# Norms of the differential heads and of the latents: sums in 128x4 columns, rows spread by PE at places of their own in the order of products

## What is computed

```
oa = diff_attention(a_q, a_k, a_v, lam, rel_bias)          # 4 heads of 128 values
oa = rms_norm(oa, da_subln[l]) * (1 - lam_init)            # a norm for each head
qm  = rms_norm(b_q,  mla_q_norm[l])  @ mla_w_qb[l]         # latent of 256
kvm = rms_norm(b_kv, mla_kv_norm[l]) @ mla_w_kvb[l]        # latent of 128
ob = mla_attention(...)        # 8 heads;   oc = sliding_window_attention(...)  # 8 heads
y = gates0 * ((oa*silu(a_z)) @ w_br_a) + gates1 * ((ob*silu(b_z)) @ w_br_b) + gates2 * (...)
x = x + rms_norm(y @ w_out[l], norm_post[l])
```

## Time and profile before

| | us |
|---|---|
| median of 3 runs | 3228.8 (3228.11 to 3232.12) |
| the profiled execution, its own time | 3226.64 |
| its span, first to last instruction | 3224.8 |
| PE busy | 3068.9 (95%) |
| DVE busy | 1882.0 (58%) |
| POOL busy, ACT busy | 1126.3, 1054.3 |
| mean granted clock of PE | 0.98 of full |

### The profile page before, as it was taken

One profiled execution on the slowest core, in us unless ns is written; L12 is line 12 of the kernel. 1 busy time (PEld: TensorE's weight loads), 2 busy tenths in 40 slices (PEclk: granted clock), 3 DMA queues, 4 the chain that ended last, 5 costly groups with the idle time before them and its releaser, 6 DMA issues.

```text
span 3224.8 us, 38645 instructions
## 1 busy us (share of the span) xinstructions
PE 3068.9 (95%) x15248; PEld 2380.1 (74%) x15248; DVE 1882.0 (58%) x3020; ACT 1054.3 (33%) x1848; POOL 1126.3 (35%) x472
## 2 busy tenths in 40 slices
PE   8989999999899999989999989999999999989998
PEld 6667777777667777767676878887677777778886
DVE  4866555465765555645533478822866666478832
ACT  4433433244343332332222232223333333332221
POOL 3322333333222334423232434443333333234442
PEclk9999999999999999999999999999999999999999
DMA  5222222232222222222121223331322222223322
GB/s 184 70 72 66 66 75 89 85 94 70 72 66 66 72 79 92 79 92 72 60 71 60 92 72 100 96 98 59 108 78 74 73 74 78 66 67 103 98 92 72
DMA packets 78760, 262.23 MB, mean 81 GB/s; under 512 B 10778, under 2 KB 13466, under 8 KB 78580
## 3 DMA queue, kind: packets, MB, share of 16 engines
q1 hardware_dynamic: 78004, 257.66, 25.4%
q10 hardware_dynamic: 576, 2.10, 0.2%
HBM read 257.56 MB, written 6.09 MB: 82 GB/s over the span
## 4 chain that ended last, share of the span: by engine, by line
PE 82%; DVE 12%; ACT 2%; issue 1%; DMA 1%; POOL 0%; SPq 0%; ACTq 0%; DVEq 0%
PE bank L668 24%; PE bank L670 23%; PE bank L669 23%; PE bank L821 2%; PE bank L774 2%; PE bank L801 1%; PE bank L957 1%; DVE x_res L1713 1%; PE bank L780 1%; ACT w_hi L1143 1%; DMA bias_copies<-bias_vectors 1%; PE bank L1005 1%; PE bank L1043 1%; POOL w_lo L535 0%; PE bank L944 0%
## 5 line engine op out<-in xcount | busy, mean ns | idle before, releaser
L535 POOL TENSOR_TENSOR w_lo<-w_raw,w_hi 128x1024 fp32r<-128x1024 f32 x462 | 1122.4, 2431 | 2043.0 <-ACT w_hi L1143 2043.0
L668 PE MATMUL bank<-h_hi,w_hi 128*128 128x512 f32 x2800 | 1151.2, 411 | 61.2 <-DVE h_lo L1701 20.4
L669 PE MATMUL bank<-h_lo,w_hi 128*128 128x512 f32 x2800 | 1106.0, 395 | 0.0
L670 PE MATMUL bank<-h_hi,w_lo 128*128 128x512 f32 x2800 | 1105.8, 395 | 0.0
L1143 ACT CAST w_hi<-w_raw 128x1024 fp32r<-128x1024 f32 x462 | 483.2, 1048 | 1272.8 <-PE bank L670 1253.3
L668 PEld LDWEIGHTS bank<-h_hi,w_hi 128*128 128x128 f32 x2800 | 534.6, 191 | 230.7 <-issue 92.5
L670 PEld LDWEIGHTS bank<-h_hi,w_lo 128*128 128x128 f32 x2800 | 532.8, 190 | 118.3
L669 PEld LDWEIGHTS bank<-h_lo,w_hi 128*128 128x128 f32 x2800 | 535.1, 191 | 104.5 <-issue 3.3
L1971 DVE TENSOR_SCALAR m<-bank,gains 128x512 f32<-128x512 f32 x48 | 36.0, 751 | 326.0 <-ACT ta L1342 193.0
L1275 ACT ACTIVATE probs<-probs,small_columns 128x128 f32<-128x128 f32 (+2 forms) x192 | 101.8, 530 | 249.0 <-DVE small_columns L1756 244.7
L669 PE MATMUL bank<-f_lo,w_hi 128*128 128x512 f32 x352 | 139.3, 396 | 0.0
(11 more groups left out here) (290 smaller groups left out, 3774.9 us busy)
## 6 DMA issues: line engine op xcount, KB each, us to landing
w_raw<-in_w SPq DMA_DIRECT2D x462, 512.0 KB, 3.5
bias_copies<-bias_vectors SPq DMA_DIRECT2D x1, 2560.0 KB
x_res<-in_x_t ACTq DMA_DIRECT2D x4, 512.0 KB, 8.0
bias<-bias_copies SPq DMA_DIRECT2D x8, 256.0 KB, 3.4
bias<-bias_copies SPq DMA_DIRECT2D x16, 128.0 KB, 2.4
out_x<-x_res SPq DMA_DIRECT2D x8, 256.0 KB, 2.0
bias_copies<-bias_vectors SPq DMA_DIRECT2D x1, 1280.0 KB
ple_raw<-in_p_t SPq DMA_DIRECT2D x2, 512.0 KB, 3.9
```

Of the source, the lines that this page charges most:

```text
L535: pool.tensor_tensor(WL[slot][:], RAW[slot][:], WH[slot][:].bitcast(F32), ALU.subtract).then_inc(sems["lo_done"], 1)
L668: pe.matmul(banks[bank][:], WH[slot][:, w], hi[:, k, :], start=start, stop=False)
L669: pe.matmul(banks[bank][:], WH[slot][:, w], lo[:, k, :], start=False, stop=False)
L670: pe.matmul(banks[bank][:], WL[slot][:, w], hi[:, k, :], start=False, stop=stop).then_inc(sems["kt_done"], 1)
```

## The change

- In `ORDER`, each of the twelve norms now has two entries of 0 steps: its sum where it was, and a new `row_da`, `row_q` or `row_kv` later in the same unit: `row_da` after q (unit 1, 2), after kr (unit 3), after g1 (unit 4); `row_q` after k (unit 2); `row_kv` after `row_da` (unit 3).
- PE: each 128x512 matmul with ones becomes `column_sums` (four matmuls of one column). At a row's entry PE runs `spread` into the next bank of three, after a wait on `inverted`.
- DVE evicts 128x4 instead of 128x512; ACT's root is on 128x4; at the start of its next share DVE takes the reciprocal of 128x4 (`inverse_inside`), which releases PE's `spread`. At the row's entry in its own order, DVE waits for `rstd_spread`, multiplies with the row read from PSUM and splits, as before.
- Each row counts as a tile: six more tiles in each `mix`.

```
@@ -68,12 +68,11 @@
 KINDS = ["da"] * 4 + ["mla"] * 4 + ["sw"] * 4
 LATENT = [("mv", 1), ("qn", 2), ("qr", 2), ("qs", 2), ("kn", 1)]
 GATES, BRANCH = [("g0", 8), ("g1", 8)], [("b0", 4), ("b1", 4)]
-DA_NEXT = [("v", 8), ("q", 8), ("k", 8)]
 ORDER = [[("bq0", 8), ("v", 8), ("z", 8), ("q", 8), ("k", 8)],
-         [("bq1", 8), ("sum_da", 0)] + DA_NEXT + [("z", 8)],
-         [("bkv", 8), ("sum_da", 0), ("sum_q", 0)] + DA_NEXT + [("z", 8)],
-         [("cv", 8), ("sum_da", 0), ("sum_kv", 0), ("ck", 8), ("turn_cv", 0), ("kr", 8), ("ks", 8)] + LATENT + [("z", 8)],
-         [("g0", 8), ("sum_da", 0), ("g1", 8), ("z", 8)] + LATENT + BRANCH,
+         [("bq1", 8), ("sum_da", 0), ("v", 8), ("q", 8), ("row_da", 0), ("k", 8), ("z", 8)],
+         [("bkv", 8), ("sum_da", 0), ("sum_q", 0), ("v", 8), ("q", 8), ("row_da", 0), ("k", 8), ("row_q", 0), ("z", 8)],
+         [("cv", 8), ("sum_da", 0), ("sum_kv", 0), ("ck", 8), ("turn_cv", 0), ("kr", 8), ("row_da", 0), ("row_kv", 0), ("ks", 8)] + LATENT + [("z", 8)],
+         [("g0", 8), ("sum_da", 0), ("g1", 8), ("row_da", 0), ("z", 8)] + LATENT + BRANCH,
          GATES + [("z", 8)] + LATENT + BRANCH,
          GATES + [("z", 8)] + LATENT + BRANCH,
          GATES + [("z", 8), ("cq", 8)] + BRANCH,
@@ -312,7 +311,7 @@
-        SM = sb("small_columns", [P, 64])
+        SM = sb("small_columns", [P, 72])
@@ -329,7 +328,6 @@
-        VARA = at("da_var", [P, SEQ], 7 * T1)
...
@@ -410,6 +408,8 @@
         MX, NM, DEN, ES, RC1, SINK, NSINK, LAMC, SUBG, ROOT = 0, 8, 16, 24, 32, 40, 48, 56, 58, 60
         INV = RC1
 
+        INSIDE = {"da": 64, "q": 68, "kv": 68}
+
         SWAP = [p + 8 if p < 8 else p - 8 if p < 16 else p for p in range(32)]
 
         def sm(c, n=1):
@@ -698,12 +698,12 @@
                                         start=(first and b == 0), stop=(last and b == QT - 1), skip_group_check=True)
                     return ins
 
-                def spread(self, bank):
+                def spread(self, bank, column=INV):
 
                     t.up("inverted")
                     pe.wait_ge(sems["inverted"], t.at("inverted"))
                     for b in range(QT):
-                        ins = pe.transpose(banks[bank][:, b * P:(b + 1) * P], sm(INV + b).to_broadcast([P, P]), ID[:])
+                        ins = pe.transpose(banks[bank][:, b * P:(b + 1) * P], sm(column + b).to_broadcast([P, P]), ID[:])
                     ins.then_inc(sems["rstd_spread"], t.one("rstd_spread"))
 
                 def mix(self, l):
@@ -723,18 +723,20 @@
                                 bank = self.rotate(3)
                                 t.up("da_squared")
                                 pe.wait_ge(sems["da_squared"], t.at("da_squared"))
-                                pe.matmul(banks[bank][:], ONES[:], SQA[:], start=True, stop=True).then_inc(sems["summed"], t.one("summed"))
+                                self.column_sums(bank, SQA).then_inc(sems["summed"], t.one("summed"))
                             elif name == "sum_q":
                                 bank = self.rotate(3)
                                 t.up("lat_squared", 2)
                                 pe.wait_ge(sems["lat_squared"], t.at("lat_squared"))
-                                pe.matmul(banks[bank][:], ONES[:], SQL[:, 0, :], start=True, stop=False)
-                                pe.matmul(banks[bank][:], ONES[:], SQL[:, 1, :], start=False, stop=True).then_inc(sems["summed"], t.one("summed"))
+                                self.column_sums(bank, SQL[:, 0, :], last=False)
+                                self.column_sums(bank, SQL[:, 1, :], first=False).then_inc(sems["summed"], t.one("summed"))
                             elif name == "sum_kv":
                                 bank = self.rotate(3)
                                 t.up("lat_squared")
                                 pe.wait_ge(sems["lat_squared"], t.at("lat_squared"))
-                                pe.matmul(banks[bank][:], ONES[:], SQL[:, 2, :], start=True, stop=True).then_inc(sems["summed"], t.one("summed"))
+                                self.column_sums(bank, SQL[:, 2, :]).then_inc(sems["summed"], t.one("summed"))
+                            elif name.startswith("row_"):
+                                self.spread(self.rotate(3), INSIDE[name[4:]])
                             else:
                                 if k == 0:
                                     self.bank = self.rotate(3)
@@ -1241,7 +1243,7 @@
                             name, k, nk = STEPS[n][self.step]
                             self.step += 1
                             self.n += nk > 0
-                            if nk and k == nk - 1 or name.startswith("sum"):
+                            if nk and k == nk - 1 or name.startswith(("sum", "row")):
                                 self.tiles += 1
                             if k == max(nk, 1) - 1:
                                 done.append((name, self.tiles))
@@ -1257,7 +1259,7 @@
                                 act.activation(SQL[:, x, :], LQ[:, x, :], ACT.Square).then_inc(sems["lat_squared"], t.one("lat_squared"))
                             elif name in ("sum_da", "sum_q", "sum_kv"):
                                 act.wait_ge(sems["evicted"], tile)
-                                v = {"sum_da": VARA[:], "sum_q": SQL[:, 0, :], "sum_kv": SQL[:, 2, :]}[name]
+                                v = sm(INSIDE[name[4:]], QT)
                                 act.activation(v, v, ACT.Sqrt).then_inc(sems["std_ready"], t.one("std_ready"))
                             elif name == "turn_cv":
                                 self.v_out(CV[:], TURN + 1)
@@ -1794,26 +1796,34 @@
                             b = {"mla": 1, "sw": 0}[KINDS[n]]
                             split(ZH[b][:, n % 4, :], ZL[b][:, n % 4, :], ZO[:], "made")
 
-                    def finish(name):
+                    def inverse_inside(name):
                         t.up("std_ready")
                         dve.wait_ge(sems["std_ready"], t.at("std_ready"))
-                        v = {"sum_da": VARA[:], "sum_q": SQL[:, 0, :], "sum_kv": SQL[:, 2, :]}[name]
-                        dve.reciprocal(v, v).then_inc(sems["dve_step"], t.one("dve_step"))
-                        dve.wait_ge(sems["dve_step"], t.at("dve_step"))
-                        if name == "sum_da":
-                            dve.scalar_tensor_tensor(ZO[:], ZO[:], sm(SUBG + l), v, ALU.mult, ALU.mult).then_inc(sems["dve_step"], t.one("dve_step"))
-                            dve.wait_ge(sems["dve_step"], t.at("dve_step"))
+                        v = sm(INSIDE[name[4:]], QT)
+                        dve.reciprocal(v, v).then_inc(sems["inverted"], t.one("inverted"))
+
+                    def finish(name, row):
+                        t.up("rstd_spread")
+                        dve.wait_ge(sems["rstd_spread"], t.at("rstd_spread"))
+                        self.tiles += 1
+                        if name == "row_da":
+                            dve.scalar_tensor_tensor(ZO[:], ZO[:], sm(SUBG + l), row, ALU.mult, ALU.mult).then_inc(sems["evicted"], 1)
+                            self.settle()
                             split(ZH[0][:, self.head, :], ZL[0][:, self.head, :], ZO[:], "made")
-                        elif name == "sum_q":
+                        elif name == "row_q":
                             for a in range(2):
                                 q = LQ[:, a, :]
-                                dve.scalar_tensor_tensor(q, q, gain(f"mlaq{l}", a), v, ALU.mult, ALU.mult).then_inc(sems["dve_step"], t.one("dve_step"))
-                                dve.wait_ge(sems["dve_step"], t.at("dve_step"))
+                                step = ("dve_step", "evicted")[a]
+                                dve.scalar_tensor_tensor(q, q, gain(f"mlaq{l}", a), row, ALU.mult, ALU.mult).then_inc(sems[step], t.one(step))
+                                if a == 0:
+                                    dve.wait_ge(sems["dve_step"], t.at("dve_step"))
+                                else:
+                                    self.settle()
                                 split(QNH[:, a, :], QNL[:, a, :], q, ("dve_step", "made")[a])
                         else:
                             q = LQ[:, 2, :]
-                            dve.scalar_tensor_tensor(q, q, gain(f"mlakv{l}"), v, ALU.mult, ALU.mult).then_inc(sems["dve_step"], t.one("dve_step"))
-                            dve.wait_ge(sems["dve_step"], t.at("dve_step"))
+                            dve.scalar_tensor_tensor(q, q, gain(f"mlakv{l}"), row, ALU.mult, ALU.mult).then_inc(sems["evicted"], 1)
+                            self.settle()
                             split(KNH[:, 0, :], KNL[:, 0, :], q, "made")
 
                     def turned_out():
@@ -1875,18 +1885,21 @@
                     def beside(n, to):
 
                         if self.pending:
-                            finish(self.pending.pop(0))
```

(8 more changed lines are left out.)

33 lines of the change are left out of this document (16 added, 17 removed).

## The result

| | before | after |
|---|---|---|
| median, us (lowest to highest, 4 runs each) | 3229.2 (3228.11 to 3232.12) | 3192.95 (3191.41 to 3193.66) |
| span of the profiled execution, us | 3224.8 | 3189.6 |
| ratio, 95% interval | | 0.9886 (0.9869 to 0.9903) |

The change gains 36.3 us where 20.2 were forecast.

A forecast was written before the change was run, and what follows sets the result against it. PE, busy 95% of the span, was taken as the bound. Terms -32.1, -5.3, +0.7, +5.3, +1.5, +7.2, +2.5 sum to -20.2 us from the profiled 3226.6; with the median 2.2 above, forecast 3208.5 us, range 3198 to 3220.

The forecast's parts named there:

- Stalls gone: PE's waits before values (28.6 us) and before turn in unit 2 (3.5 us) go: 32.1 us less.
- The clock behind them: PE's lower clock after the gaps of units 1 and 3 goes with those gaps: 5.3 us less, bounds 0 and 5.3.
- Column sums: On PE, a column sum takes 0.90 us against 0.85 for a sum with ones; fourteen give +0.7 us.
- Spreads: Twelve new spreads on PE at 0.44 us each, none hidden, +5.3 us; the wait for inverted costs nothing.
- DVE's lateness: Later product and split delay DVE, chiefly maxima of block 3 in unit 3: +1.5 us, bounds 0 and 10.
- The join: Where linear begins, six more tiles make PE wait for b1's eviction: +7.2 us, and +2.5 us for the clock.
- The moved stall of unit 3: Splits meet POOL, DVE is late for maxima of block 3, PE stands 5 us a layer: 3218.5 us, chance 0.17.
- The harmless join: The start of linear costs nothing because ACT's gate or DVE comes earlier: 9.7 us less, 3199 us, chance 0.10.
- The cheap sums: Column sums' weight loads hide behind a product on PE, 0.6 us less for each of 14: 3200 us, chance 0.03.
- the weights: ACT's casts come late and PE waits at chunk starts: 3223 to 3229 us, chance 0.06.
- the standing at the rows: PE's waits for inverted before the spreads hold all products, so the change is slower: 3236 us, chance 0.04.

The follow-up runs named there:

- runs 1, 2 and 4: In turn: kernel before with small_columns 72 wide, 3210.92 us; kernel before with 80, 3231.75 us; changed kernel with 80 instead of 72, 3212.36 us.
- run 12: The changed kernel with two unused 32-byte tiles, putting h_hi and h_lo 32 above a multiple of 64 and everything behind 64 bytes later; 3221.98 us.
- run 8: The kernel before, arena moved 32 bytes, with the wide finish (reciprocal, product, split) moved to the places of the changed kernel's rows; 3203.76 us.
- after_pad32: The changed kernel with small_columns 80 wide instead of 72, its arena again 32 above a multiple of 64; 3212.36 us.
- both join kernels: The changed kernel with linear after each mixer opening banks 3, 4, 5 (3178.03 us) or banks 1, 2, 3 (3184.67 us).
- h_moved: The changed kernel with h_hi and h_lo moved to 32 above a multiple of 64 by two unused tiles; 3221.98 us.
- run 9: The changed kernel with each of the twelve spreads written four times over into the same bank; 3204.99 us.
- Run 6: The changed kernel with linear opening banks 1, 2, 3, as the kernel before did; 3184.67 us.
- before_pad64: The kernel before with small_columns 80 wide instead of 64, its arena 64 bytes later; 3231.75 us.
- before_pad32: The kernel before with small_columns 72 wide instead of 64, its arena 32 bytes later at a multiple of 64; 3210.92 us.
- run 3: The kernel before with small_columns 88 wide, its arena at 117440, a multiple of 64 but not of 128; 3216.68 us.
- after_join345: The changed kernel with linear after each mixer opening banks 3, 4, 5; 3178.03 us.

## Why the prediction was wrong, and where it was right

**The step that failed is a part missing from the sum.** The working went through reciprocals, sums, spreads and even the running count of the banks, "which the change does not mention", and passed over the one line that only makes `small_columns` eight columns wider. It was costed at nothing without being named. It moves every tile behind it by 32 bytes, and by runs 1, 2 and 4 that is worth 18.6 us in the kernel before and 19.4 in the kernel after. It could have been asked of the trace of before: products on h and products on f are the same instruction, and their durations were 389 and 396 ns (run 12's last row, and the first `f_hi` row above).

With the address kept equal, the change gains 17 to 19 us (run 4) against 20.2. So the mechanism that was forecast is there, and the time missed the range because a second one, as large, came with it. Part by part:

1. Stalls gone, 32.1 us: before `values` 29.4 fell to 1.2, so 28.2 of the 28.6, and the 1.75 us before `turn` are gone in both mixers. The margin in unit 1 is 1.15 us, not the 0.6 that I worked out. By run 8 the late place alone takes these stalls away but makes others, which the narrow form avoids.
2. The clock behind them, 5.3 us: full in both stretches of the earlier trace rows, as said. But the column sums of unit 2 bring a fall of their own in some executions, which the sum held at nothing. Over both mixers the lower clock took 8.4 to 10.6 us of PE's work in the four traces of the kernel before, padded or not, and 3.4 to 5.1 in the five that have after's mixer (after, after_pad32, both join kernels, h_moved). By the means, 9.3 and 4.8, the term is -4.5.
3. Column sums: 0.90 us each, as said. By the page "TensorE: Matmul & The Clock Gate" of the Trainium skill, section "Back-to-back issue gap", with its floor of 25 ns for a matmul of so few columns, a sum would have been 0.2 us, an estimate; the trace does not agree here. It shows eight weight loads for each sum; that they set its pace was argued in the prediction and has no run of its own.
4. Spreads: 0.45 us each by the neighbours, no wait before them; run 9 gives 0.33 to 0.44.
5. DVE's lateness, +1.5 us: not seen. The wait for qs is 2.6 us in each mixer as before, and that before `values` does not grow. The term should have been about 0.
6. The join, +9.7 us: PE stands 6.50 us instead of 2.97, so +7.1 for two layers. The clock: after, 5 us at the lower level, 2.5 us lost in each layer; before, none in the first and, with 0.66 granted over the 5 us from 1263, 1.7 in the second. That is +3.3, in all +10.4. Run 6, which restores the old banks, gives 8.3.

These corrected terms give -31.7 - 4.5 + 0.7 + 5.3 + 0 + 10.4 = -19.8, one to three us more than the runs show (with the 8.3 of run 6 in the last place, -21.9). Two executions of the same code differ by as much: the traces of after and after_join345 have the same instructions up to the join, and PE reaches it at 563.8 and at 566.8 us. In after the mean clock was 0.97 from 20 to 80 us and 1.00 behind that; in after_join345 it was 1.00 from 20 to 80 and 0.97 in two stretches of 60 us between 140 and 500. So the remainder is not put down to a cause.

**The rivals.** The moved stall of unit 3 did not come. The harmless join did not come either: the 3192.95 us lie nearer its 3199 than the forecast's 3208.5 and could have been taken for it from the time alone, but the trace has the 6.5 us. The cheap sums are refuted by the spacing, the weights and the standing at the rows by the waits. That the time fell below the range came from none of them.

## What to carry to other kernels

Read the diff for what it allocates as well as for what it computes: any buffer that changes its size moves all that lie behind it, and 32 bytes were worth as much here as the whole rewrite of the norms. Test it apart, by padding the kernel before by the same amount. And where a running count picks buffers, work out what a new entry does at the next place that reads the count; choosing banks whose last eviction is old gave another 15 us for a few lines.

## What the runs showed of the hardware

- An fp32r matmul of 128x512 took 0.233 us from start to start with its moving operand in SBUF 32 bytes above a multiple of 64, and 0.226 to 0.227 on a multiple of 128, 3% less at the same full clock. That is the stage of products on f in before, before_pad64 and after, before_pad32. The arena's move by 32 bytes was worth 18.6 us; moving h off by 32, with the rings and the arena 64 further, cost 29.
- What lies between is not settled. With the arena at 117440, a multiple of 64 but not of 128, run 3 took 120.2 us for the f stage; in run 12 the arena lay at the same address and f ran at 389 ns and 119.0 us, with the weight rings 64 bytes further too. So the address of the moving operand alone doesn't decide that last part; how the rings' place enters was not tried. In the mixers not every product followed either: those on h, at a multiple of 128 in before and in after, were at 397 ns by the median of L668 in both.
- A gap of 6.5 us on PE was followed by 5 us at the lower clock in both layers, one of 2.97 us by none in the first layer of before and by some 3 us in run 6, though not at once: the spacing there was 0.23 us for the first five matmuls and 0.43 for the next seven.
- Three groups of column sums back to back (24 matmul records of one column, 2.6 us, no idle time) ended within 0.7 us of a fall to the lower clock, 3.4 us long, in 11 of 18 places over nine traces (786.6 to 790.0 in after); the wide sums in their place, in none of 10 over five. No run separates them from the products around them, so that they are the cause is likely but not shown.
- Sixteen transposes of a broadcast column cost 1.75 us more than none, four 0.45: they add up evenly at 0.11 us each.
